# Prompt attention with its weights laid out in strips by ScalarE and VectorE and turned in 32x32 blocks, in place of TensorE transposes

## The reference

```python
def fox_prompt(q, k, v, logf):            # S=1024, 8 heads x 64, Q_BLOCK=128
    c = jnp.cumsum(logf, axis=1).transpose(0, 2, 1)
    # for each block of 128 queries:
    s = jnp.einsum('bqhd,bkhd->bhqk', qi, k).astype(jnp.float32) * scale
    s = s + ci[..., :, None] - c[:, :, None, :]
    s = jnp.where(pi[:, None] >= key_pos[None, :], s, -jnp.inf)
    p = jax.nn.softmax(s, axis=-1)
    return jnp.einsum('bhqk,bkhd->bqhd', p.astype(v.dtype), v)
```

## Time and profile before

| what | value |
|---|---|
| median of 3 runs | 1885.07 us (1884.13 to 1886.02) |
| span of the profiled execution | 1884.4 us |
| mean granted TensorE clock | 0.976 |
| busy share of the span: PE / PEld / DVE / ACT / POOL | 94% / 49% / 31% / 16% / 10% |
| prompt attention within the span | 344.4 to 706.8 us |

### The profile page before, as it was taken

The page is one execution under the profiler, slowest core; times in us unless marked ns, Lnnn a source line. Parts: engine busy times, 40 slices in busy tenths (PEclk is TensorE's granted clock), DMA queues, the critical chain, the costliest instruction groups (busy, mean ns, idle before and its releaser), DMA issues. The chain is left out here.

```text
span 1884.4 us, 23119 instructions
## 1 busy us (share of the span) xinstructions
PE 1780.2 (94%) x8719; PEld 916.1 (49%) x8719; DVE 577.3 (31%) x1154; ACT 309.1 (16%) x552; POOL 197.0 (10%) x309
## 2 busy tenths in 40 slices
PE   7999999899999997988799989999999999995997
PEld 4564554555566663444564445444444444442443
DVE  4301114333434354655222236111111111110565
ACT  1000001222223233322200114100000000000122
POOL 2000004200000002333100000100000000000330
PEclk9999999999999998999999998999999999998999
DMA  7012110344444529998722146899999999996342
GB/s 284 5 22 82 48 51 1 115 154 157 140 137 158 191 95 338 369 377 315 289 77 81 68 167 248 334 405 417 419 428 418 418 424 422 418 424 232 107 150 67
DMA packets 133089, 426.46 MB, mean 226 GB/s; under 512 B 24217, under 2 KB 62682, under 8 KB 120690
## 3 DMA queue, kind: packets, MB, share of 16 engines
q1 hardware_dynamic: 98242, 327.59, 45.6%
q0 software_dynamic: 19136, 66.63, 9.6%
q10 hardware_dynamic: 15600, 30.75, 4.3%
HBM read 374.14 MB, written 50.79 MB: 225 GB/s over the span
## 5 line engine op out<-in xcount | busy, mean ns | idle before, releaser
L2233 PE MATMUL psum<-arena 128*64 128x512 f32 (+1 forms) x1024 | 341.1, 595 | 1.4 <-DVE arena L2327 1.4
L902 PE MATMUL psum<-arena 128*128 128x384 f32 (+1 forms) x768 | 253.9, 476 | 3.9 <-ACT arena L933 3.9
L2233 PEld LDWEIGHTS psum<-arena 128*64 128x64 f32 (+1 forms) x1024 | 129.0, 163 | 179.1 <-issue 177.3
L902 PEld LDWEIGHTS psum<-arena 128*128 128x128 f32 x768 | 139.6, 191 | 77.5 <-issue 5.8
L2272 PE MATMUL psum<-arena 128*64 128x512 f32 (+1 forms) x512 | 171.7, 603 | 1.0 <-DVE arena L2341 1.0
L2272 PEld LDWEIGHTS psum<-arena 128*64 128x64 f32 (+1 forms) x512 | 66.6, 165 | 103.1 <-issue 103.1
L2592 PE MATMUL psum<-arena 128*128 128x512 f32 x256 | 113.7, 602 | 1.4 <-DVE arena L2618 1.4
L1692 PE MATMUL psum<-arena 128*128 128x512 f32 x256 | 113.0, 596 | 1.6 <-PEq L1513 1.6
L317 PE MATMUL psum<-arena 128*128 128x512 f32 x256 | 112.8, 598 | 0.0
L2327 DVE TENSOR_TENSOR arena<-psum,g_moe_rows 128x1024 f32<-128x1024 f32 x24 | 29.4, 1224 | 252.0 <-PE psum L2227 252.0
L2592 PEld LDWEIGHTS psum<-arena 128*128 128x128 f32 x256 | 48.8, 193 | 60.1 <-issue 60.1
(11 more groups left out here) (301 smaller groups left out, 1864.3 us busy)
## 6 DMA issues: line engine op xcount, KB each, us to landing
arena<-in_w_exp_gate SPq DMA_DIRECT2D x32, 2048.0 KB, 13.5
arena<-in_w_exp_up SPq DMA_DIRECT2D x32, 2048.0 KB, 14.1
arena<-in_w_exp_down SPq DMA_DIRECT2D x32, 2048.0 KB, 10.5
arena<-in_cache_v POOLq DMA_DIRECT2D x128, 256.0 KB, 9.1
arena<-in_cache_k SPq DMA_DIRECT2D x124, 256.0 KB, 9.5
arena<-in_w_in SPq DMA_DIRECT2D x24, 1024.0 KB, 6.1
moe_out<-arena ACTq DMA_DIRECT2D x24, 512.0 KB, 11.8
arena<-in_w_in SPq DMA_DIRECT2D x5, 2048.0 KB, 19.9
```

Source lines behind the costliest of these rows:

```text
L902: done = mm(c.bank[7][:, 0:b - a], WG[blk % 2][:, k, q * P:(q + 1) * P], HT[p // NCOL][:, k, :], start=(k == 0), stop=(k == KD - 1))
L2233: last = mm(out[rows_, :], XT[:, u % 2, k, rows_], c.ring_tile(LOAD[kind, u, r])[:, k, :], start=(k == 0), stop=(k == KD - 1))
```

## The change

TensorE no longer transposes. Each head's tile of weights is written into PT by 16 instructions of 32 partitions: the source is 32 queries (strip q, partitions 32q to 32q+31) and, of every key block, 32 keys (s); the destination is partitions 32s to 32s+31, columns 32q to 32q+31 of each block. The multiplication by one over the sum is done on the way. VectorE writes q = 0, 1 and ScalarE q = 2, 3, eight instructions each for a head. Then one VectorE instruction for a head turns all 32x32 blocks of its PT in place. On TensorE an iteration is now `scores(m)`, `weigh(m-2)`, three gate halves without a break; `weigh` alternates banks 6 and 4, the gate pieces banks 7 and 5. On ScalarE a `keep_gate` stands between the strips of the two heads, and both `exp` come behind them.

```diff
+    def cell(m, hl, q, s):
+        n = m % NP + 1
+        w = S[SW * q:SW * q + SW, m % 2, hl, 0:n * P].rearrange("p (k s d) -> p s k d", s=STRIPS, d=SW)[:, s]
+        return w, PT[SW * s:SW * s + SW, m % 2, hl, 0:n, SW * q:SW * q + SW]
 # TensorE
             def weigh(m):
-                pe.wait_ge(ev_a, parts_before(m + 1))
-                pe.wait_ge(ev_b, parts_before(m + 1))
-                if m >= 1:
-                    pe.wait_ge(at_ev, m)
+                pe.wait_ge(turned, 2 * m + 2)
+                if m >= 2:
+                    pe.wait_ge(at_ev, m - 1)
...
-                    if p >= 1:
-                        pe.wait_ge(gate_ev, p)
+                    if p >= 2:
+                        pe.wait_ge(gate_ev, p - 1)
...
             for m in range(N + 2):
                 if m < N:
                     scores(m)
-                    gate_half(3 * m)
-                if m % 2 and 2 <= m:
-                    weigh(m - 2)
-                if 1 <= m <= N:
-                    turn(m - 1, 0)
-                if m < N:
-                    gate_half(3 * m + 1)
-                if 1 <= m <= N and (m - 1) % NP >= 4:
-                    turn(m - 1, 1)
-                if m % 2 == 0 and 2 <= m:
+                if m >= 2:
                     weigh(m - 2)
                 if m < N:
-                    gate_half(3 * m + 2)
+                    for g in range(3):
+                        gate_half(3 * m + g)
 # ScalarE
+            def lay(m, hl):
+                act.wait_ge(rc, 2 * m + hl + 1)
+                if m >= 2:
+                    act.wait_ge(pv, m - 1)
+                for q in (2, 3):
+                    for s_ in range(STRIPS):
+                        w, out = cell(m, hl, q, s_)
+                        s.activation(out, w, ACT.Copy, scale=inv[SW * q:SW * q + SW, m % 4, hl:hl + 1]).then_inc(laid_a, 1)
             for m in range(N + 1):
+                if m >= 2 and m % 2 == 0:
+                    keep_gate(3 * m // 2 - 1)
+                if m >= 1:
+                    lay(m - 1, 0)
                 if m < N:
+                    keep_gate((3 * m - 1) // 2 if m % 2 else 3 * m // 2)
+                if m >= 1:
+                    lay(m - 1, 1)
+                if m < N:
                     exp(m, 0)
                     exp(m, 1)
...
 # VectorE
+            def lay(m, hl):
+                dve.wait_ge(rc, 2 * m + hl + 1)
+                if m >= 2:
+                    dve.wait_ge(pv, m - 1)
+                for q in (0, 1):
+                    for s in range(STRIPS):
+                        w, out = cell(m, hl, q, s)
+                        v.tensor_scalar(out, w, inv[SW * q:SW * q + SW, m % 4, hl:hl + 1], None, ALU.mult).then_inc(laid_v, 1)
+            def turn(m, hl):
+                dve.wait_ge(laid_v, CELLS * (2 * m + hl + 1))
+                dve.wait_ge(laid_a, CELLS * (2 * m + hl + 1))
+                weights = PT[:, m % 2, hl, 0:m % NP + 1, :].rearrange("p k n -> p (k n)")
+                v.transpose(weights, weights).then_inc(turned, 1)
             for m in range(N + 2):
                 if m < N:
                     bias(m)
-                    scale(m, 0)
                 if 1 <= m <= N:
-                    keep(m - 1, 0)
+                    lay(m - 1, 0)
+                    lay(m - 1, 1)
+                    turn(m - 1, 0)
+                    turn(m - 1, 1)
+                if 2 <= m <= N:
+                    keep_out(m - 2)
                 if m < N:
-                    scale(m, 1)
-                if 1 <= m <= N and (m - 1) % NP >= 4:
-                    keep(m - 1, 1)
-                if m >= 2 and m <= N:
-                    keep_out(m - 2)
+                    invert(m, 0)
+                    invert(m, 1)
```

More of the change, by code:

```diff
@@ L739, in stage_prompt_attention @@
     s_mm, ttr, low_done, exps = c.sem("s_mm"), c.sem("s_biased"), c.sem("s_low"), c.sem("exps")
-    rc, scaled = c.sem("inv_done"), c.sem("p_scaled")
-    tr_a, tr_b, ev_a, ev_b = c.sem("p_tr_a"), c.sem("p_tr_b"), c.sem("p_ev_a"), c.sem("p_ev_b")
+    rc, laid_v, laid_a, turned = c.sem("inv_done"), c.sem("p_laid_dve"), c.sem("p_laid_act"), c.sem("p_turned")
+    STRIPS = 4
+    SW = P // STRIPS
+    CELLS = STRIPS * STRIPS // 2
     pv, at_ev = c.sem("pv"), c.sem("at_ev")
@@ L886, in weigh @@
                         r = slice(hl * DH, (hl + 1) * DH)
-                        done = mm(c.bank[6][r, 0:P], V[:, k, (2 * pr + hl) * DH:(2 * pr + hl + 1) * DH],
+                        done = mm(c.bank[6 - 2 * (m % 2)][r, 0:P], V[:, k, (2 * pr + hl) * DH:(2 * pr + hl + 1) * DH],
                                   PT[:, m % 2, hl, k, :], start=(k == 0), stop=(k == i))
@@ L898, in gate_half @@
                         pe.wait_ge(wg_in[blk % 2], 16 * (blk // 2 + 1))
-                    if p >= 1:
-                        pe.wait_ge(gate_ev, p)
+                    if p >= 2:
+                        pe.wait_ge(gate_ev, p - 1)
                 for k in range(4 * (g % 2), 4 * (g % 2) + 4):
-                    done = mm(c.bank[7][:, 0:b - a], WG[blk % 2][:, k, q * P:(q + 1) * P], HT[p // NCOL][:, k, :],
+                    done = mm(c.bank[7 - 2 * (p % 2)][:, 0:b - a], WG[blk % 2][:, k, q * P:(q + 1) * P], HT[p // NCOL][:, k, :],
                               start=(k == 0), stop=(k == KD - 1))
@@ L932, in keep_gate @@
                     act.wait_ge(c.gate_out[p % NRAW], 16 * (p // NRAW))
-                s.activation(RAW[:, p % NRAW, 0:b - a], c.bank[7][:, 0:b - a], ACT.Copy).then_inc(gate_ev, 1)
+                s.activation(RAW[:, p % NRAW, 0:b - a], c.bank[7 - 2 * (p % 2)][:, 0:b - a], ACT.Copy).then_inc(gate_ev, 1)
             def exp(m, hl):
@@ L988, in bias @@
                 if m >= 2:
[L989 to L992, removed]
+                    dve.wait_ge(laid_a, 2 * CELLS * (m - 1))
+                    dve.wait_ge(laid_v, 2 * CELLS * (m - 1))
                 for q, (half, bank, a, b, _) in enumerate(parts(m)):
@@ L1006, in bias, with invert @@
                     dve.sem_inc(low_done, 1)
-            def scale(m, hl):
-                w = (m % NP + 1) * P
+            def invert(m, hl):
                 dve.wait_ge(exps, 2 * m + hl + 1)
                 v.reciprocal(inv[:, m % 4, hl:hl + 1], total[:, m % 4, hl:hl + 1]).then_inc(rc, 1)
+            def lay(m, hl):
                 dve.wait_ge(rc, 2 * m + hl + 1)
[L1013 to L1019, removed]
                 if m >= 2:
                     dve.wait_ge(pv, m - 1)
-                v.tensor_copy(PT[:, m % 2, 1, k0:k1, :], c.bank[5][:, 0:(k1 - k0) * P].rearrange("p (k n) -> p k n", n=P)
-                              ).then_inc(ev_b, 1)
+                for q in (0, 1):
[7 more added lines that the diff above has]
+                v.transpose(weights, weights).then_inc(turned, 1)
             def keep_out(m):
                 dve.wait_ge(pv, m + 1)
-                v.tensor_copy(AT[:, m % NP, m // NP, :], c.bank[6][:, 0:P]).then_inc(at_ev, 1)
+                v.tensor_copy(AT[:, m % NP, m // NP, :], c.bank[6 - 2 * (m % 2)][:, 0:P]).then_inc(at_ev, 1)
             for m in range(N + 2):
```

18 lines of the change are left out of this document (removed).

## The result

The changed kernel takes 1902.55 us (median of 4 runs, 1897.94 to 1907.44), the kernel before 1884.6 (4 runs): 1.0092 times as long, 95% interval 1.0073 to 1.0112. The forecast was 1887.7 with a range of 1868 to 1899, so it was wrong: the change costs 18 us by medians, and 13.2 by the spans of the two profiled executions (1884.4 and 1897.6; the latter's own time is 1899.23). What follows compares spans and places in the trace.

The account below looks back on a forecast made before the run. The prediction took PE to bound the prompt attention. Its terms, -35.4 off PE, +27.3 waits, +12.5 tail and -1.8 next stage, sum to +2.6 us on the 1884.4 span: 1887.0, as median 1887.7, range 1868 to 1899.

Parts of the forecast that it names:

- Off PE, -35.4: Prompt attention, ahead of the last gate half's end: transposes and waits for bank 7 leave PE, 35.4 us saved.
- The strips: Spacing of the new 32-partition copies at n = 8: 0.383 us on DVE, 0.53 on ACT, none overlapping.
- the two voices: DVE spacing evidence: L483s start 0.085 us before the last ends; L449 starts 0.03 late, read as held by changed destination partitions.
- The waits, 27.3: Prompt attention: PE's weigh waits for DVE's turns, 27.3 us over odd and even tiles together.
- A: Odd tiles: weigh waits because ACT's keep_gate stands ahead of the second head's strips; 13.4 us over the stage.
- B: Even tiles: weigh waits for exps behind ACT's strips, then DVE's bias, strips and turns, or key turns; 13.9 us.
- Its clock is already full, so longer gate stretches have nothing to win there.: PE in the prompt attention: granted clock 0.98 and 1.00 of 2.4 GHz, so no gain from longer gate stretches.
- The tail, +12.5: From the last gate half to the stage's last copy: 19.5 us instead of 7.0, so 12.5 more.
- The next stage, -1.8: Stage after the prompt attention: its wait of 1.84 us for keys is over, 1.8 us saved.
- Overlapping strips: Rival: strips start before the last ends, 0.27 us on DVE, 0.41 on ACT; 1866.5 us, chance 0.25.
- DVE at one element a cycle: Rival: strided DVE strips take 0.45 us instead of 0.383; 1895 us, 1901 with slower ACT strips; chance 0.22.
- Doing other than it says, 1860: Rival: waits sit elsewhere, PE keeps pace but for the tail, if ACT's keep_gate doesn't hold strips; 1860 us, chance 0.05.

Follow-up runs that it names:

- x4_both: Changed kernel with weigh(m-2) behind the first gate half and ScalarE's keep_gate behind both exps; 1863.8 us, ratio 0.9892 to the kernel before.
- x1_fill: Changed kernel with idle PE products in place of waiting at the three changes of pair and in the tail; 1889.61 us, ratio 1.0027 to the kernel before.
- x0_after: The changed kernel again, with no edit, as base for the runs beside it; 1900.61 us, ratio 1.0094 to the kernel before.
- x3_copy_last: Changed kernel with ScalarE's keep_gate moved from between the two heads' strips to behind both exps; 1868.47 us, ratio 0.9913 to the kernel before.

## Why the prediction was wrong

*Off PE, -35.4.* Right: 34.4 by x4_both.

*The strips.* Right. DVE starts 0.375 us apart at n = 8 (16 in 5.98), 0.383 were taken; ACT 0.528 (8 in 4.20), 0.53 were taken. For DVE there is luck in it. L449 was read as a copy that starts late because it writes other partitions than L447. In the kernel it writes the same 64 partitions, reads others (64 to 127), and waits for a semaphore that L447 raises, so its 0.03 us could not tell the two voices apart and is no evidence for the rule named there. L1344 could, for ACT: its copies each write other partitions than the one before, with no wait between them.

*The waits, 27.3.* Right in sum (26.2) and, but for one, in their places. One by one, forecast and measured: n = 2 0 and 0.22, n = 4 0.3 and 0.48, n = 6 0.6 and 0.75, n = 8 2.6 and 2.73; n = 7 2.3 and 1.98, narrow 3.5 and 3.26. Beside the key turns 0.7 + 1.9 + 3.2 were forecast and 0.80, none and 2.77 measured: the weigh of n = 3 at 659.99 does not wait. The closeness of the sum is partly luck, for A was too small (13.4, measured 15.2) and B too large (13.9, measured 11.0). A wait of 2.0 us of a gate half for its weights (in_w_in) is new and was not forecast.

*"Its clock is already full, so longer gate stretches have nothing to win there."* **This is the step that failed.** It is nearly true of the kernel before, but the sum that follows puts eight waits of 1.9 to 3.5 us into the stage and prices each at its own length; the slower products behind them stand in the sum at nothing, and no reason is given. The clock was only asked what it could win, never what it could lose. It lost 12.7 us ahead of the last gate half, and x1_fill, which fills the waits at the changes of pair, takes the loss there away (11.0 of them are at the changes of pair; the 1.7 behind the wait of 2.77 came in this execution and not in x0_after). The trace of the kernel before had shown the case, once:

```profile
352.56 4.54 PE L902 MATMUL psum<-arena 128*128 128x384 f32 x8 [2.24 <-ACT arena L933]
```

```profile
352.00:356.00 4.00, 3.44 (x7) 1.96 (x8) 0.63 (x3) 0.51 (x3) 0.00 (x0) 0.68 0.93 346
```

Behind a wait of 2.24 us a gate half takes 4.54 us instead of 2.80. That is where the 0.98 of the earlier trace rows comes from, and it was read as a full clock. The changed kernel's profile has no such loss in its first tile, which makes 1.7 us in its favour. The first part then adds up to -35.4 + 26.2 + 2.0 + 12.7 - 1.7 = +3.8, against +3.9 measured. About 1 us of that agreement is chance, as the stage began 0.9 us earlier (343.47 against 344.39).

*The tail, +12.5.* Right in size (+13.1), and in part by luck: two waits of 6 and 7 us were in the chain of steps, but the slow clock behind them (3.26 + 3.68 against 1.75 + 1.97, 3.2 us) was not, and other steps were priced a little high.

*The next stage, -1.8.* Some 3.7 came back: the wait for keys (1.84) and about as much again in the rest of the span, where the stages that follow are the same in both kernels. The rest is within what two executions differ by: from the stage's last copy to the end x0_after takes 1175.7 us and this one 1173.9.

*The rivals.* Overlapping strips: none overlap. DVE at one element a cycle: its time, 1895 to 1901, is near the measured one and its cause is wrong, since 256 elements take 0.344 us and not 0.45. Doing other than it says, 1860: nearly the time of x4_both, and in part for the reason that it named, that the copy must not hold the strips (x3_copy_last, that edit alone, is at 1868.47); but this kernel has the copy where it does. The rival that was missing is the forecast case with the clock at 1.2 GHz behind its long waits.

*The marks set beforehand.* Waits, strips and tail came out as they should; "the stage's end within 5 us of 706.8" did not (723.7), and it was the one that the clock touches.

By medians 14.9 us are missing from the forecast, by spans 10.6; the changed kernel's runs spread over 9.5 us, the kernel before over 2.

## What to carry to other kernels

When work moves from the busiest engine to others, its average load there matters less than what stands next to it in each list: here one gate half ahead of weigh, or one copy moved behind the exps, turned 0.9% slower into 0.85% faster, and both together gave 1.1 to 1.3% faster than the kernel before. Put a long independent piece between a late producer's release and its consumer, and keep entries that wait for a third engine out of the middle of a producer's run. Price a new wait of 2 to 3 us on TensorE at its length plus what the lower clock takes from the work behind it. Here the seven waits of 2 to 3.3 us, 18.6 us in all, cost 12.7 more in one execution and 10.1 in another: half to two thirds of their length, and as much again at the worst change of pair.

## What the runs showed of the hardware that was not expected

- Two waits of 1.98 and 2.73 us, 13 us apart, with full work between them, each brought the granted clock to 0.57 and 0.50 in the slice of 4 us behind it; 4.7 us of waiting cost 4.5 more. It is not so every time: in x0_after the same two waits cost 1.5, with a clock of 1.00 behind the second. The same times filled with idle products kept it at 1.00, and the kernel was 11 us faster for it.
- DVE's strips of an odd number of blocks last as long as those of the next even one: 343 ns for 7 blocks and 344 for 8, 309 and 313 for 5 and 6, 280 and 276 for 3 and 4 (but 233 and 245 for 1 and 2). The forecast took fewer elements to be quicker (0.366 us apart for n = 7); 16 strips in 5.96 us are 0.374 apart.
- ACT's strips don't overlap, like DVE's: 0.528 us apart at a length of 0.503, in either order of the strips. The Trainium skill, "ScalarE: Activation LUTs", section "What ACT_TABLE_LOAD costs", has back-to-back ones overlap by about 93 ns, measured on 128 partitions. The exps of this trace agree with it (L927 starts at 425.16 and lasts 1.15, and its read of the row sum starts at 426.21, 0.10 before that ends). The strips of 32 partitions don't, and for them the measurement decides.
